# Product-key experts: the first product of a key in 512 and 256 columns, a VectorE sum of its halves, and another order of the work around the activation

## The reference

```
h     = rms_norm(x, g_ffn)                       # 256 tokens x 1024
hid   = gelu(h @ peer_u.T)                       # 256 x 16384
x    += (hid * g) @ peer_v                       # 256 x 1024
```

## Time and profile before

| what | value |
|---|---|
| median of 3 executions | 2835.95 us |
| the profiled execution | 2838.09 us |
| its span, first to last instruction | 2836.4 us |
| TensorE busy | 2541.9 us, 90% |
| VectorE busy | 1108.7 us, 39% |
| ScalarE busy | 665.5 us, 23% |
| mean granted TensorE clock | 0.959 |
| first product of the experts' stage | 518.07 us |
| last product of the experts' stage | 1241.47 us |

### The profile page before, as it was taken

One profiled execution on the slowest core, in us unless ns is written; L12 is line 12 of the kernel. 1 busy time (PEld: TensorE's weight loads), 2 busy tenths in 40 slices (PEclk: granted clock), 3 DMA queues, 4 the chain that ended last, 5 costly groups with the idle time before them and its releaser, 6 DMA issues. The chain is left out here.

```text
span 2836.4 us, 41079 instructions
## 1 busy us (share of the span) xinstructions
PE 2541.9 (90%) x15952; PEld 1793.5 (63%) x15952; DVE 1108.7 (39%) x2340; ACT 665.5 (23%) x1237; POOL 123.8 (4%) x180
## 2 busy tenths in 40 slices
PE   8988987899999999989888799998867979998896
PEld 6647756799999999967855454444335645544442
DVE  1231989666666666634522311111126232111112
ACT  2120129544444444423201100000013111000000
POOL 1020000000000000000200000000002000000000
PEclk9999999999999999999989899999979989999998
DMA  5314420355555555563053499999931525999996
GB/s 198 130 42 163 146 108 0 119 185 192 181 189 188 182 192 183 187 239 137 33 209 126 172 427 427 427 427 427 407 116 45 237 83 249 428 426 427 427 426 255
DMA packets 130021, 649.57 MB, mean 229 GB/s; under 512 B 15443, under 2 KB 25046, under 8 KB 95446
## 3 DMA queue, kind: packets, MB, share of 16 engines
q1 hardware_dynamic: 118080, 627.80, 55.9%
q10 hardware_dynamic: 11814, 19.96, 2.1%
HBM read 641.43 MB, written 6.29 MB: 228 GB/s over the span
## 5 line engine op out<-in xcount | busy, mean ns | idle before, releaser
L459 PE MATMUL banks<-weight_ring,window_rows_T 128*64 128x256 f32 x2496 | 287.0, 384 | 39.4 <-DMA weight_ring<-in_moe_w_up 31.9
L459 PE MATMUL banks<-peer_input_high,u_high 128*128 128x256 f32 x1024 | 291.2, 284 | 4.5 <-DVE u_low L1506 4.4
L2792 DVE COPY expert_hidden_T<-banks 128x256 f32<-128x256 f32 x64 | 27.2, 425 | 677.2 <-PE banks L2651 677.2
L459 PE MATMUL banks<-peer_input_high,u_low 128*128 128x256 f32 x1024 | 291.4, 285 | 0.0
L459 PE MATMUL banks<-peer_input_low,u_high 128*128 128x256 f32 x1024 | 291.3, 284 | 0.0
L459 PEld LDWEIGHTS banks<-weight_ring,window_rows_T 128*64 128x64 f32 x2496 | 188.9, 138 | 151.3 <-DMA weight_ring<-in_moe_w_up 43.3
L459 PEld LDWEIGHTS banks<-peer_input_high,u_high 128*128 128x128 f32 x1024 | 197.5, 193 | 10.3 <-DVE u_low L1506 5.5
L1474 PE MATMUL banks<-v_high,gated_high 128*128 128x512 f32 x512 | 201.1, 393 | 0.0
L1474 PE MATMUL banks<-v_low,gated_high 128*128 128x512 f32 x512 | 201.0, 393 | 0.0
L459 PEld LDWEIGHTS banks<-peer_input_low,u_high 128*128 128x128 f32 x1024 | 197.4, 193 | 4.7
L1474 PE MATMUL banks<-v_high,gated_low 128*128 128x512 f32 x512 | 199.5, 390 | 0.0
(11 more groups left out here) (460 smaller groups left out, 3514.0 us busy)
## 6 DMA issues: line engine op xcount, KB each, us to landing
weight_ring<-in_moe_w_down SPq DMA_DIRECT2D x42, 2048.0 KB, 35.4
weight_ring<-in_moe_w_gate SPq DMA_DIRECT2D x40, 2048.0 KB, 34.6
weight_ring<-in_moe_w_up SPq DMA_DIRECT2D x38, 2048.0 KB, 34.4
v_of_key<-in_peer_v_rows SPq DMA_DIRECT2D x128, 512.0 KB, 3.5
x<-in_peer_u_T SPq DMA_DIRECT2D x128, 512.0 KB, 4.2
more_weight_slots<-in_moe_w_up SPq DMA_DIRECT2D x26, 2048.0 KB, 32.9
more_weight_slots<-in_moe_w_gate SPq DMA_DIRECT2D x24, 2048.0 KB, 35.2
more_weight_slots<-in_moe_w_down SPq DMA_DIRECT2D x22, 2048.0 KB, 35.0
```

The source lines that it names most:

```text
L459: return k.nc.tensor.matmul(out, lhsT, rhs, start=start, stop=stop)
L2792: nc.vector.tensor_copy(b.hid_T[:, e % 2, :, :].rearrange("p m n -> p (m n)"), k.ps[:, TURN_BANK, 0:2 * P]).then_inc(k.turned_copied.up(), 1)
```

## The change

The two parts of the layer's input become one tile, `peer_input_high_low` of 128 x 8 x 2 x 256. In pre, one product of 512 columns (`u_high` with both parts) takes the place of two of 256, so the bank holds two halves that have still to be added; the product of `u_low` with the high part adds into the first half. VectorE gets a new part, `add`: it copies the second half from PSUM to `key_sums` and adds the first half to it; gelu reads `key_sums`. The buffer `gated` is single now, with a wait of its own. The orders change: in step n ScalarE makes u_high(n + 3) first, then gelu(n + 1) and v_high(n + 1); VectorE makes add(n + 1), u_low(n + 3), then gate(n + 1) and v_low(n + 1). Ahead of the loop VectorE has add(0) before gate(0). SyncE's block is the same as before.

```diff
@@ pre
             if not start:
-                pe.wait_ge(k.act_ready.sem, k.act_ready.at(n - 3))
-            out = k.ps[:, 4 + b, 0:S]
+                pe.wait_ge(k.key_sums_ready.sem, k.key_sums_ready.at(n - 3))
+            out = k.ps[:, 4 + b, :]
             for ch in range(DC):
                 high, low = (as_u(t, b % 2)[:, ch, :] for t in parts[0])
-                h_high, h_low = hT_high[:, ch, :], hT_low[:, ch, :]
-                mm(k, out, high, h_high, ch == 0, False)
-                mm(k, out, high, h_low, False, False)
-                last = mm(k, out, low, h_high, False, ch == DC - 1)
+                nc.tensor.matmul(out, high, hT_both[:, ch, :, :].rearrange("p a t -> p (a t)"), start=ch == 0, stop=False,
+                                 skip_group_check=True)
+                last = nc.tensor.matmul(out[:, 0:S], low, hT_both[:, ch, 0, :], start=False, stop=ch == DC - 1,
+                                        skip_group_check=True)
@@ act_gelu
-            act.wait_ge(k.products.sem, k.products.at(n + 1))
+            act.wait_ge(k.key_sums_ready.sem, k.key_sums_ready.at(n + 1))
...
-            nc.scalar.activation(gelu[:, b % 2, :], k.ps[:, 4 + b, 0:S], ACT.Gelu).then_inc(k.act_ready.up(), 1)
+            nc.scalar.activation(gelu[:, b % 2, :], total[:, b % 2, :], ACT.Gelu).then_inc(k.act_ready.up(), 1)
@@ new
+        def add(dve, n, b, start):
+
+            dve.wait_ge(k.products.sem, k.products.at(n + 1))
+            if not start:
+                dve.wait_ge(k.act_ready.sem, k.act_ready.at(n - 1))
+            nc.vector.tensor_copy(total[:, b % 2, :], k.ps[:, 4 + b, S:2 * S]).then_inc(k.halves_copied.up(), 1)
+            dve.wait_ge(k.halves_copied.sem, k.halves_copied.at(n + 1))
+            nc.vector.tensor_tensor(total[:, b % 2, :], k.ps[:, 4 + b, 0:S], total[:, b % 2, :],
+                                    ALU.add).then_inc(k.key_sums_ready.up(), 1)
@@ gate
-            nc.vector.tensor_tensor(w[:, b % 2, :], gelu[:, b % 2, :], g, ALU.mult).then_inc(k.dve_step.up(), 1)
+            if not start or n:
+                dve.wait_ge(k.weights_gated.sem, k.weights_gated.at(n))
+            nc.vector.tensor_tensor(w[:, :], gelu[:, b % 2, :], g, ALU.mult).then_inc(k.dve_step.up(), 1)
@@ act_step
+            if i is not LAST or b + 3 < TURN:
+                i3, b3 = later(3)
+                high(act, 0, n + 3, i3, b3, i is FIRST and b + 3 < 2)
             if i is not LAST or b + 1 < TURN:
                 i1, b1 = later(1)
                 act_gelu(act, n + 1, b1, i is FIRST and b + 1 < 2)
                 high(act, 1, n + 1, i1, b1, i is FIRST and b + 1 < 2)
-            if i is not LAST or b + 3 < TURN:
-                i3, b3 = later(3)
-                high(act, 0, n + 3, i3, b3, i is FIRST and b + 3 < 2)
@@ dve_step
             n = TURN * i + b
             if i is not LAST or b + 1 < TURN:
+                add(dve, n + 1, (b + 1) % TURN, i is FIRST and b + 1 < 2)
+            if i is not LAST or b + 3 < TURN:
+                low(dve, 0, n + 3, (b + 3) % TURN)
+            if i is not LAST or b + 1 < TURN:
                 gate(dve, n + 1, (b + 1) % TURN, i is FIRST and b + 1 < 2)
                 low(dve, 1, n + 1, (b + 1) % TURN)
-            if i is not LAST or b + 3 < TURN:
-                low(dve, 0, n + 3, (b + 3) % TURN)
@@ the vector block, ahead of the loop
             low(dve, 0, 0, 0)
             low(dve, 0, 1, 1)
+            add(dve, 0, 0, True)
             gate(dve, 0, 0, True)
```

More of the change, by code:

```diff
@@ L257, in __init__ @@
         self.x_in_banks = signal("x_in_banks")
+        self.halves_copied = signal("halves_copied")
+        self.key_sums_ready = signal("key_sums_ready")
         self.scores_ready = signal("scores_ready")
@@ L1389, in _ @@
                 dve.wait_ge(k.act_ready.sem, k.act_ready.at(1))
-                nc.vector.tensor_tensor(hT_low[:, :, :], hT[:, :, :], hT_high[:, :, :],
+                nc.vector.tensor_tensor(hT_low, hT[:, :, :], hT_high,
                                         ALU.subtract).then_inc(k.dve_step.up(), 1)
@@ L1413, in _ @@
                 act.wait_ge(k.small_loaded.sem, k.small_loaded.at(16))
-                nc.scalar.activation(hT_high[:, :, :], hT[:, :, :], ACT.Copy).then_inc(k.act_ready.up(), 1)
+                nc.scalar.activation(hT_high, hT[:, :, :], ACT.Copy).then_inc(k.act_ready.up(), 1)
                 with act.Fori(1, turns) as i:
@@ L1426, in load_key, with peer_experts, peer_steps @@
     sp.dma_start(raw[which][:, b, :], src).then_inc(k.key_landed[which][b], 16)
-def peer_experts(k, gates, raw, hT_high, hT_low):
+def peer_experts(k, gates, raw, hT_both):
     with ExitStack() as c:
         parts = [[k.sb(f"{m}_{n}", [P, 2, D], F32R, ctx=c) for n in ("high", "low")] for m in "uv"]
-        gelu, w = (k.sb(n, [P, 2, S], ctx=c) for n in ("gelu_out", "gated"))
+        gelu, total = (k.sb(n, [P, 2, S], ctx=c) for n in ("gelu_out", "key_sums"))
+        w = k.sb("gated", [P, S], ctx=c)
         w_high, w_low = (k.sb(n, [P, 2, S], F32R, ctx=c) for n in ("gated_high", "gated_low"))
-        peer_steps(k, gates, raw, parts, hT_high, hT_low, gelu, w, w_high, w_low)
-def peer_steps(k, gates, raw, parts, hT_high, hT_low, gelu, w, w_high, w_low):
+        peer_steps(k, gates, raw, parts, hT_both, total, gelu, w, w_high, w_low)
+def peer_steps(k, gates, raw, parts, hT_both, total, gelu, w, w_high, w_low):
     nc = k.nc
@@ L1516, in gate @@
                                     ALU.mult).then_inc(k.dve_step.up(), 1)
-            nc.vector.tensor_tensor(w[:, b % 2, :], gelu[:, b % 2, :], g, ALU.mult).then_inc(k.dve_step.up(), 1)
+            if not start or n:
+                dve.wait_ge(k.weights_gated.sem, k.weights_gated.at(n))
+            nc.vector.tensor_tensor(w[:, :], gelu[:, b % 2, :], g, ALU.mult).then_inc(k.dve_step.up(), 1)
             dve.wait_ge(k.dve_step.sem, k.dve_step.at(2 * n + 2))
-            nc.vector.tensor_tensor(w_low[:, b % 2, :], w[:, b % 2, :], w_high[:, b % 2, :],
+            nc.vector.tensor_tensor(w_low[:, b % 2, :], w[:, :], w_high[:, b % 2, :],
                                     ALU.subtract).then_inc(k.weights_gated.up(), 1)
@@ L1594, in _ @@
                     dve_step(dve, i, b)
-            for sig in (k.weights_gated, k.u_low_ready, k.v_low_ready):
+            for sig in (k.weights_gated, k.u_low_ready, k.v_low_ready, k.halves_copied, k.key_sums_ready):
                 sig.repeated(turns - 2, TURN)
@@ L1622, in first_block @@
         raw = [x, sb("v_of_key", [P, 2, D], ctx=c)]
-        hT_high, hT_low = (sb(f"peer_input_{n}", [P, DC, S], F32R, ctx=c) for n in ("high", "low"))
-        peer_gates(k, slots_T, gates, raw, hT_high, hT_low, hT_keep)
-        peer_experts(k, gates, raw, hT_high, hT_low)
+        hT_both = sb("peer_input_high_low", [P, DC, 2, S], F32R, ctx=c)
+        peer_gates(k, slots_T, gates, raw, hT_both[:, :, 0, :], hT_both[:, :, 1, :], hT_keep)
+        peer_experts(k, gates, raw, hT_both)
     k.stream = k.streams[1]
```

## The result

The change makes the kernel slower: 3357.14 us (median of 4, 3349.91 to 3361.46) against 2836.09 us for the kernel before (median of 4 here), a ratio of 1.184 with a 95% interval of 1.1815 to 1.1858. The forecast was 3345 us, the range 3285 to 3405. The profiled execution took 3356.69 us, with a span of 3354.9.

The account below looks back on a forecast made before the run. TensorE bounds the kernel before; after the change a loop of waits through SyncE's loads does, 9.70 us a key. +511.3 (steps) + 0.9 (start) - 2.7 (end) = +509.5 us, so 3345 us against the median, range 3285 to 3405.

Parts of the forecast that it names:

- The bound and the second loop: Experts' stage: TensorE sets 5.62 us a key; waits through SyncE, ScalarE and VectorE, 9.70 us, go from two keys to one.
- ScalarE's part: ScalarE's new order: gelu(n + 1) and v_high(n + 1) queue behind u_high(n + 3), but don't set the end.
- The size of a step: v_low to v_low in the stage: 9.70 us, of which 5.11 from v_low's end to u_high; 125 steps, +511.3 us.
- Rival C: Same loop, another landing time of u: steps of 9.24 to 10.2 us, 3288 to 3406; 90 in 100 for the loop.
- The end and the start: Stage's ends: add(0) delays v_low(0) by 0.9 us; last product some 11.2 us behind v_low(125) for 13.9, so -2.7 us.
- The wide product: Pre on TensorE: 8 of 24 products fewer, 0.08 us per key, 10 us in 128 keys, counted as nothing here.
- Rival A: SyncE's queue: the loop doesn't close and TensorE sets the pace; -9.5 us, 2826 us; 4 in 100.
- add: VectorE's two added instructions, 0.9 us a key, hidden while it waits for u; bounds 0 and 0.9, taken as 0.
- The clock: TensorE in the stage: mean clock well below 1; a slow pre 5.1 us, with post 7.9, inside 9.70; cost 0.
- TensorE waiting for u_low some 4 us a key: Sign in the stage of the forecast being right: TensorE stands still about 9.70 - 5.54 = 4.2 us in each key.
- Rival B: TensorE at 1.2 GHz becomes the stage's bound: 10.2 us a key, +65 us, 3410 us; 5 in 100.

Follow-up runs that it names:

- the changed kernel's second trace: The changed kernel, with nothing altered, run again on another chip than its first runs: 3341.72 us, the traced execution 3339.33 us.

## Why the prediction was right

*The bound and the second loop.* Right. The loop was hidden at 4.85 us a key under TensorE's 5.62, it is now paid once per key, and it falls away with either half of its cause: at SyncE's order alone (2830.57 us), and at the two orders alone (2843.83 us, and 2830.64 without add). With only one of the two orders undone it stays closed, as the prediction's text on ScalarE's part implies.

*The size of a step.* 9.70 forecast, 9.81 measured. Put the measured distance, 5.23 us, in place of 5.11, and the sum is 5.23 + 1.09 + 1.14 + 0.34 + 0.45 + 0.34 + 1.22 = 9.81; every other term held to 0.01 us. It is the landing that grew, for u was issued 0.72 us behind v_low in the mean both before and after: 4.3 us in the median for 4.2. Between the profiled executions the forecast of 3347.6 became 3356.7 by 14.2 us in the 125 steps, -1.2 at the start, -0.9 at the end and -3.0 behind the stage, where the forecast had nothing. Rival C had the landing as the open term, and had guessed that loads further apart would land sooner. They didn't: 5.11 us before, 5.09 to 5.23 in the six traces in which the loop closes once per key with SyncE's order as it was. That the mean of the kernel before would hold was assumed, not argued. The share of distances over 5.3 us was 38% before, 42% after and 27% in the changed kernel's second trace, and these last two differ by 17 us. That the forecast lies within 12 us of the one median and 3 of the other is in part luck; the range covered the open term.

*The end and the start.* The last product came 1763.03 - 1752.72 = 10.3 us behind v_low(125), forecast 11.2; most of the rest is pre(127), 1750.51 to 1754.96, which took 4.45 us for the 5.1 of a slow one. v_low(0) ended 0.3 us earlier than before, not 0.9 later: add(0) cost its 0.9, but the stage began 1.3 us sooner (u_low(0) at 515.50 for 516.79).

*The wide product.* The price of 0.08 us a key was near what pre gained, 0.06 to 0.07 us, or 8 ns for each of the 8 products fewer, though the 229 ns for 512 columns came from the post. What it left out is the post, which takes 0.03 to 0.04 us longer in all four kernels with the wide product in which TensorE is busy throughout, so 0.026 us a key are left, 3.3 ns for each product fewer. By the 2.5 ns that the Trainium skill (TensorE: Matmul & The Clock Gate, Part 1) gives as the fixed part of a warm product it would be 0.02 us a key: the whole key comes near that, pre by itself does not. It made no difference to the forecast. Rival A would have been too low: its case, measured with u's loads ahead, came to 2.8 us below the kernel before, not 9.5.

*add.* Right for this kernel: no cost beside a wait of 5 us. The sentence on its bounds was wrong: "if that cover were gone, 0.9 us a key is added to VectorE's 3.7, still under 5.6" counts VectorE's throughput. With both orders back the cover was gone and add cost 13 us, since it lengthened the loop over two keys past TensorE's time. The right bound was the loop's slack, 2 x 5.62 - 9.70 = 1.54 us over two keys, which add with the handover to gelu and on to the gate, 0.45 + 0.48 + 0.57 = 1.50, uses up once the distance is 5.26 and not 5.11.

*The clock.* The mean is 0.85 in the stage. TensorE was slow for part of its bursts: a pre took 4.07 us in the mean and 5.3 at most, where 5.1 was assumed for a slow one. It was still done before the next u_low: with the loop as bound, terms without the clock give the step to 0.01 us. The sign "TensorE waiting for u_low some 4 us a key" was too high, since it took a burst at the full clock: TensorE stood still for 339 of 1210 us, 2.7 us a key. Rival B, TensorE as bound, would have shown it busy throughout.

*Rival A* decided as said: its point was the loop under 5.54 us, and once SyncE's order let u go ahead, so that its load was under way before v_low(n) ended, the kernel came to 2830.57.

## What to carry to other kernels

Where several engines work in written orders that run ahead of each other, follow each ring of waits once around, count over how many steps it closes, and divide: moving one instruction from the end of a step to its front can leave every engine's work the same and halve that number. A load queue that serves two streams in turn ties them together; issue each load when its own buffer is free, before any reordering behind it. And an instruction added beside an idle engine is free only if it is in no ring, or if the ring has the slack for it and for the handovers around it.

## What was not expected of the hardware

The distance from the end of v_low to the start of u_high differs between executions by more than all other terms together: 5.23 us in one, 5.09 in another of the same kernel, the landing 4.3 and 4.2 us in the median, with u issued 0.72 us behind v_low in both. Of two loads of 512 KB issued about 0.5 to 0.9 us apart the second lands in 4.2 to 4.3 us and the first in 3.5, whichever tile it is for: v lands in 3.5 and u in 4.3 in the changed kernel, u in 3.5 and v in 4.3 with the two exchanged. Where the two went out 2.6 to 3 us apart, in the changed kernel with u's loads ahead, both landed in 3.5.
